# Two attention stages of a two-block kernel: where the scores of the item after next stand in TensorE's order

## What is computed

```python
# first block: differential attention, 4 heads, 16 leading meta columns, value width 128
attn = softmax(q1 k1^T / sqrt(d), causal) - lam * softmax(q2 k2^T / sqrt(d), causal)
o = attn @ v
# second block: forgetting attention, 8 heads, value width 64
logits = q k^T / sqrt(d) + c[query] - c[key]      # causal
o = softmax(logits) @ v
```

## Time and profile before

| What | us |
|---|---|
| median of 3 runs | 2825.19 (2814.3 to 2830.16) |
| the profiled execution's own time | 2824.86 |
| its span in the profile | 2823.1 |
| first attention, about | 336 to 519.7 |
| second attention, about | 1742.8 to 1907.5 |
| PE busy, of the span | 2562.9 |
| DVE, ACT, POOL busy | 1055.8, 522.0, 912.2 |

### The profile page before, as it was taken

The page is one execution under the profiler, slowest core; times in us unless marked ns, Lnnn a source line. Parts: engine busy times, 40 slices in busy tenths (PEclk is TensorE's granted clock), DMA queues, the critical chain, the costliest instruction groups (busy, mean ns, idle before and its releaser), DMA issues.

```text
span 2823.1 us, 30676 instructions
## 1 busy us (share of the span) xinstructions
PE 2562.9 (91%) x12294; PEld 2073.5 (73%) x12294; DVE 1055.8 (37%) x1624; ACT 522.0 (18%) x1001; POOL 912.2 (32%) x571
## 2 busy tenths in 40 slices
PE   8996577389999999999999998885999999999997
PEld 7875455277788888788878886774778878878885
DVE  5982556443522222222254511664342222222224
ACT  4220144512200000000023002443220000000001
POOL 3210120014633333333364452000463333333332
PEclk9998789679999999999999998996999999999998
DMA  4545600003311111111132212000321111111113
GB/s 135 139 144 125 197 30 1 4 30 112 105 45 45 46 45 45 46 45 45 45 135 68 61 53 97 1 1 23 128 82 45 45 46 45 45 46 45 45 45 127
DMA packets 184652, 184.39 MB, mean 65 GB/s; under 512 B 38440, under 2 KB 150952, under 8 KB 183616
## 3 DMA queue, kind: packets, MB, share of 16 engines
q1 hardware_dynamic: 173856, 164.18, 18.9%
q10 hardware_dynamic: 10656, 18.19, 2.0%
HBM read 149.75 MB, written 32.59 MB: 65 GB/s over the span
## 4 chain that ended last, share of the span: by engine, by line
PE 84%; ACT 4%; DVE 4%; DMA 2%; issue 2%; POOL 2%; SPq 1%; ACTq 0%; POOLq 0%; DVEq 0%
PE ps L269 24%; PE ps L271 24%; PE ps L270 24%; PE ps L1451 3%; PE ps L1481 3%; PE ps L1467 2%; ACT ex L1528 2%; DMA us_b<-ud 1%; DVE hbuf L515 1%; DVE hbuf L521 1%; PE ps L546 1%; DMA yd<-yb 1%; PE ps L1456 1%; DVE hbuf L1812 1%; PE ps L2235 1%
## 5 line engine op out<-in xcount | busy, mean ns | idle before, releaser
L1801 DVE TENSOR_TENSOR mlp_f<-mlp_f,ps 128x1024 f32<-128x1024 f32 x44 | 53.7, 1221 | 835.7 <-PE ps L271 806.1
L209 POOL TENSOR_TENSOR wgt<-raw,ones 128x512 fp32r<-128x512 f32 x76 | 86.6, 1140 | 808.9 <-PE ps L271 636.9
L1670 POOL TENSOR_TENSOR mlp_w2h<-mlp_raw,ones 128x1024 fp32r<-128x1024 f32 x44 | 83.3, 1894 | 814.8 <-PE ps L271 730.3
L1812 DVE TENSOR_TENSOR hbuf<-hbuf,ps 128x1024 f32<-128x1024 f32 x176 | 214.8, 1220 | 241.9 <-PE ps L271 241.9
L269 PE MATMUL ps<-mlp_w2h,mlp_fh 128*128 128x512 f32 x704 | 279.8, 397 | 10.2 <-issue 7.4
L269 PE MATMUL ps<-xh,mlp_w0h 128*128 128x512 f32 x704 | 279.0, 396 | 7.7 <-ACT mlp_f L1782 5.1
L269 PE MATMUL ps<-xh,mlp_w1h 128*128 128x512 f32 x704 | 278.8, 396 | 2.8 <-DVE xl L535 2.8
L271 PE MATMUL ps<-mlp_w2h,mlp_fl 128*128 128x512 f32 x704 | 279.1, 396 | 0.0
L270 PE MATMUL ps<-mlp_w2l,mlp_fh 128*128 128x512 f32 x704 | 278.9, 396 | 0.0
L271 PE MATMUL ps<-xh,mlp_w1l 128*128 128x512 f32 x704 | 278.6, 396 | 0.0
L270 PE MATMUL ps<-xl,mlp_w0h 128*128 128x512 f32 x704 | 278.5, 396 | 0.0
(11 more groups left out here) (384 smaller groups left out, 4764.4 us busy)
## 6 DMA issues: line engine op xcount, KB each, us to landing
mlp_raw<-in_w_ffn_in SPq DMA_DIRECT2D x44, 512.0 KB, 4.3
h<-hbuf SPq DMA_DIRECT2D x24, 512.0 KB, 2.9
mlp_raw<-in_w_gate SPq DMA_DIRECT2D x22, 512.0 KB, 4.3
mlp_raw<-in_w_up SPq DMA_DIRECT2D x22, 512.0 KB, 5.3
mlp_raw<-in_w_down SPq DMA_DIRECT2D x22, 512.0 KB, 4.4
mlp_raw<-in_w_ffn_out SPq DMA_DIRECT2D x22, 512.0 KB, 4.1
raw<-in_w_in SPq DMA_DIRECT2D x40, 256.0 KB, 2.7
raw<-in_w_out SPq DMA_DIRECT2D x32, 256.0 KB, 2.7
```

What stands on the lines that cost most here:

```text
L209: nc.gpsimd.tensor_tensor(wh[:, s, :], r, ones[:, 0:1].broadcast_to([P, 512]), ALU.mult).then_inc(w_hi, 1)
L1670: nc.gpsimd.tensor_tensor(self.sh[j][:, b, :], self.raw[:, j, :], ones[:, 0:1].broadcast_to([P, D]), ALU.mult).then_inc(self.s[f"hi{j}"], 1)
L1801: v.tensor_tensor(self.f[:, :], self.f[:, :], ps[:, 2:4, :].rearrange("p b c -> p (b c)"), ALU.mult).then_inc(self.s["prod"], 1)
L1812: v.tensor_tensor(self.acc[:, i, :], self.acc[:, i, :], ps[:, b:b + 2, :].rearrange("p b c -> p (b c)"), ALU.add)\
```

## The change

`pe` no longer issues the scores of item n+2 ahead of everything else of item n when item n has several batches. It issues them after the turn of the second batch and the value products of the first. Items with one batch keep the old order, and so does the second head of a pair in the second attention, which issues no scores. Nothing else is changed: the other engines' orders, buffers, waits and the instructions themselves are the same.

```diff
--- before.py
+++ after.py
@@ -1497,12 +1497,16 @@
                 self.pe_scores(pe, 1)
             self.pe_turn(pe, 0)
             for n in range(len(self.items)):
-                if n + 2 < len(self.items) and (self.maps == 2 or n % 2 == 0):
+                ahead = n + 2 < len(self.items) and (self.maps == 2 or n % 2 == 0)
+                several = self.first[n + 1] - self.first[n] > 1
+                if ahead and not several:
                     self.pe_scores(pe, n + 2)
                 for b in range(self.first[n], self.first[n + 1]):
                     if b + 1 < len(self.batches):
                         self.pe_turn(pe, b + 1)
                     self.pe_pv(pe, b)
+                    if ahead and several and b == self.first[n]:
+                        self.pe_scores(pe, n + 2)
 
         def evacuate(self, eng, cp, b):
             n, tiles = self.batches[b]
```

## The result

The changed kernel takes 2831.73 us (median of 16 runs, 2827.25 to 2838.99), the kernel before 2820.21 us (16 runs beside them, 2813.3 to 2830.16). The ratio is 1.0043, 95% interval 1.0034 to 1.0053: about 12 us slower. The profiled execution of the changed kernel is the slowest of its 16 (2838.99 us, span 2837.1), so its total says 7 us too much; what can be read from it are periods and waits.

What follows compares the result with a forecast made beforehand. No single engine bounds either attention; each runs in a loop through several. From 2824.86, first attention -11.8, clock -3.0 and second attention +12.8 gave 2822.9, written 2823 us, with nearly everything between 2808 and 2840.

Steps and rivals of the forecast that it cites:

- First attention, the path: First attention: moved turn and values fill PE's idle time ahead of scores; 11.8 us off, bounds 6 to 14.
- Gain from two rows: First attention, i3 to i5: second exponential starts 0.10 us after DVE's maximum ends, gaining 0.92, 0.88 and 0.84 us.
- The clock: First attention: half-clock stretches in the first head disappear as waits shrink; 3.0 us off.
- both falls: First head, PE at half clock from 375.5 to 378.6 and 385.7 to 388.6, costing 1.6 and 1.4 us.
- 3 us on: Clock term's unfavourable end: the other attention or other items may fall to half clock instead.
- Second attention: the path: Second attention: later scores delay DVE's maximum and B's evacuation; 3.2 us a group, 12.8 us on, bounds 0 to 18.
- the walk through DVE's queue: Second attention, i4 to i6: delays at B's evacuation and A's values add 1.27, 1.0 and 0.9 us; i7 adds nothing.
- the third rival: Second attention: PE's clock falls behind 12 new waits, 1.5 us each, 18 us on top, total 2841; chance 0.09.
- between 1800 and 1825: Second attention: granted clock leaving 1.00 in this time span would decide for the clock-fall rival.
- My sum: Whole kernel: 2824.86 - 11.8 - 3.0 + 12.8 = 2822.9, written as 2823 us.
- The first attention gains nothing: First attention: DVE's maxima or the exponentials fully take the evacuation's place; total 2838; chance 0.11.
- the end of the maxima: First attention: DVE's maxima end about 1 us before the exponential starts, given against the no-gain rival.

Runs made afterwards that it cites:

- the first experiment: New order in the first attention only, the second as before; against the kernel before 0.9989 (0.9974 to 1.0005), 3 us faster.
- fitted fillers: New order, first attention only, plus unread small matmuls sized to PE's waits: 0.9955 of the kernel before; with the new order in both attentions, 0.9994.
- The second attention alone: New order in the second attention only, the first as before; against the kernel before 1.0063 (1.0044 to 1.0083), 18 us slower.

## Why the prediction was wrong

The range held the time; the direction did not: 2 us faster was forecast, with a chance of 0.11 for slower by more than 0.5%, and it came out 0.43% slower.

**First attention, the path: right.** "Gain from two rows" for i3 to i5, nothing in i6, 0.42 us in i7 make 3.06 us a head, 37.8 instead of 40.86. Undisturbed heads take 37.80 (one of the first experiment, all with fitted fillers). On the path the order alone is worth what was said.

**The clock: the step that failed.** "With the change these waits shrink to about half [...] I take both falls as gone: 3.0 us off." The waits did shrink to half and the falls did not go: the changed kernel's heads of 40.49 and 40.75 us are 2.7 and 3.0 us over the path's 37.80, and with the new order in the first attention alone the heads are 1.3, 0 and 3.2 us over it. I had read two falls behind waits of 2.1 us as a thing of long waits, and had overlooked the third, at 402.5; but the two later heads wait as long (2.15 us ahead of the scores at 455.11 and 461.46) and keep full clock, so the rows before did not show that the wait's length decides. What the later heads showed was one pattern of waits and work that repeats after 40.86 us and holds full clock; the new pattern is another one and mostly does not. My lower bound for this term was "3 us on"; against the forecast path it is about 9 us on (11.8 expected, 3 measured in the first attention alone). Filling the waits brings heads of 37.8 to 38.9 us back, in three kernels. By the Trainium skill's rule (TensorE: Matmul & The Clock Gate, "HAM oscillation — how this bites in real kernels") bursts with waits between them fall again and again. The traces agree in part: 0.52 granted behind 1.84 us of waiting, but one head in three of the first experiment kept full clock. As I cited it, the rule says that waits bring falls and not that waits half as long bring none, so it gave no ground for my 3.0 us.

**Second attention: the path right, a little small.** 3.2 us a group forecast, 3.44 measured, 12.8 against 13.8 us. Counted from the moved turn of i4 (1803.58 in the changed kernel), each point of the walk through DVE's queue comes 0.15 to 0.25 us later than I gave it. The falls there (the third rival, at 0.09) came in part. The changed kernel has two, at 1764.5 and 1897.5, and not between 1800 and 1825 where I had said to look; the one that a period holds costs 2.4 us. If the other costs as much, 4 x 3.44 and 2 x 2.4 us make the 18.6 us by which this attention is longer in that trace. The second attention alone has one such group, and is 18 us slower and not 14. My sum had nothing for these falls.

**The forecast as a whole.** My two path terms alone make 1.0 us slower (12.8 - 11.8), by the measured periods 2.0. The forecast of "faster" rested on the 3.0 us of the clock term alone, and that term had the wrong sign in the first attention, while falls in the second stood in the sum with nothing. With fillers in the first attention both parts add up to 0.9994 of before, 1.7 us faster. That this is near the 2 us of my sum is partly luck: the interval goes from 6 us faster to 2 us slower, the fillers are worth 6 us even in the old order where I had counted 3.0 for the falls, and in the one trace of that kernel the second attention kept full clock without fillers, which the changed kernel's did not. "The first attention gains nothing" was among the rivals, with its time of 2838, but for another cause; the end of the maxima that I gave against it was right.

**Still open.** Why a given pattern of waits lets the clock fall and another does not was not tested beyond fillers against none. And heads say more than totals. From first scores to last output the first attention took 178.9 to 183.7 us in the five profiled runs that have the old order in it without fillers, 169.0 to 175.0 in the three with the new order alone, and 163.3 and 162.6 with fitted fillers. So the new order alone shortens this stage by about 8 us in the traces and 3 us in the medians, with fitted fillers by about 18 and 12.7. All that is outside the two attentions, the same instructions in all kernels, took from 2471.6 to 2483.5 us in the 13 profiled runs, so a single profile can mislead by as much as the difference; whether it does, no run tells.

## What to carry over

When an order on PE is changed, price the clock with the waits: with single waits of up to 1.84 us in a head, the same order took 37.8 or 41 us a head, and up to 1.05 us of matmuls of no use in a wait kept the 37.8. A gain that is forecast from a fall going away needs a row that shows that it goes. Fit such fillers to the wait, since those that reached past it cost 1.1 us a head. And before moving a piece of PE work out from between two others, ask which evacuation it covers: where the evacuating engine has its own long work that the move delays, as DVE's maximum here, both delays were paid on PE.

The version to keep has the new order in the first attention only, with fitted fillers: 0.9955 of the kernel before.

## What was not expected of the hardware

Stretches at half clock were of unlike length (375.5 to 378.6 before, 460.5 to 467.5 after), and PE was busy all through both: it was not idleness inside them that kept the clock down. And the same instructions, at the same place of consecutive heads, got full clock in one head and half in the next (37.80 and 40.95 us), while in the kernel before two heads in a row were alike within 0.01 us.
